# The one-hots of eight tokens: three VectorE operations over 1024 columns instead of nine small ones on VectorE and four on POOL

## What is computed

```python
def peer_ffn(h, wq, subkeys, u_tab, v_tab):
    q = (t @ wq).reshape(ntok, 8, 2, 128)
    sc = jnp.einsum('thpd,hpkd->thpk', q, subkeys)
    s1, i1 = lax.top_k(sc[:, :, 0], 16)
    s2, i2 = lax.top_k(sc[:, :, 1], 16)
    cand = (s1[..., :, None] + s2[..., None, :]).reshape(ntok, 8, 256)
    best, pos = lax.top_k(cand, 16)
    e1 = jnp.take_along_axis(i1, pos // 16, axis=-1)
    e2 = jnp.take_along_axis(i2, pos % 16, axis=-1)
    idx = e1 * 128 + e2
    gate = jax.nn.softmax(best, axis=-1)
    ...
    act = jax.nn.gelu(jnp.einsum('phkd,pd->phk', u_tab[ib], tb)) * gb
    return jnp.einsum('phk,phkd->pd', act, v_tab[ib])
```

## Time and profile before

| | us |
|---|---|
| median of 3 runs (lowest, highest) | 4073.61 (4067.85, 4075.52) |
| the profiled execution, its own time | 4059.55 |
| its span, first to last instruction | 4057.7 |
| PE busy in it | 3913.6 |
| DVE busy | 2264.8 |
| ACT busy | 1470.3 |
| POOL busy | 866.5 |

### The profile page before, as it was taken

One profiled execution on the slowest core, in us unless ns is written; L12 is line 12 of the kernel. 1 busy time (PEld: TensorE's weight loads), 2 busy tenths in 40 slices (PEclk: granted clock), 3 DMA queues, 4 the chain that ended last, 5 costly groups with the idle time before them and its releaser, 6 DMA issues. The chain is left out here.

```text
span 4057.7 us, 55604 instructions
## 1 busy us (share of the span) xinstructions
PE 3913.6 (96%) x22292; PEld 3412.3 (84%) x22292; DVE 2264.8 (56%) x3948; ACT 1470.3 (36%) x2122; POOL 866.5 (21%) x780
## 2 busy tenths in 40 slices
PE   8999999999899999999899999999999999999998
PEld 7987799999785668788677886699999999999998
DVE  4434446554544445555557543367997665666665
ACT  3253335222325344422355343333333333333333
POOL 1000012112100002211103500026656553111100
PEclk9999999999999999999999999999999999999999
DMA  3111132222110113222122121236656778888874
GB/s 130 61 39 42 42 115 94 90 93 89 58 64 35 50 52 128 91 96 97 63 89 63 32 94 55 87 112 215 221 172 203 248 247 290 281 265 265 266 251 138
DMA packets 232559, 519.42 MB, mean 128 GB/s; under 512 B 36272, under 2 KB 134704, under 8 KB 231920
## 3 DMA queue, kind: packets, MB, share of 16 engines
q1 hardware_dynamic: 160288, 399.71, 29.8%
q0 software_dynamic: 18432, 67.12, 4.7%
q10 hardware_dynamic: 53584, 49.04, 3.6%
HBM read 454.66 MB, written 60.82 MB: 127 GB/s over the span
## 5 line engine op out<-in xcount | busy, mean ns | idle before, releaser
L304 PE MATMUL PSM<-UX,PARTS 128*128 128x264 f32 (+3 forms) x3392 | 1184.0, 349 | 44.1 <-DVE UX L333 24.9
L305 PE MATMUL PSM<-UX,PARTS 128*128 128x264 f32 (+3 forms) x3392 | 1164.9, 343 | 0.0
L306 PE MATMUL PSM<-UX,PARTS 128*128 128x264 f32 (+3 forms) x3392 | 1161.4, 342 | 0.0
L272 DVE TENSOR_TENSOR PARTS<-RAW,PARTS 128x1024 fp32r<-128x1024 f32 x549 | 686.0, 1256 | 600.4 <-ACT PARTS L262 545.8
L262 ACT ACTIVATE PARTS<-RAW 128x1024 fp32r<-128x1024 f32 x612 | 644.9, 1056 | 991.6 <-PE PSM L306 485.7
L304 PEld LDWEIGHTS PSM<-UX,PARTS 128*128 128x128 f32 x3392 | 645.1, 190 | 130.7 <-DVE UX L333 34.7
L305 PEld LDWEIGHTS PSM<-UX,PARTS 128*128 128x128 f32 x3392 | 645.7, 190 | 59.1 <-issue 2.9
L306 PEld LDWEIGHTS PSM<-UX,PARTS 128*128 128x128 f32 x3392 | 644.9, 190 | 59.0
L2591 PE MATMUL PSM<-AC,PARTS 128*128 128x448 f32 x1024 | 375.3, 366 | 2.0 <-DVE AC L2850 2.0
L2593 PE MATMUL PSM<-AC,PARTS 128*128 128x448 f32 x1024 | 374.6, 366 | 0.0
L2592 PE MATMUL PSM<-AC,PARTS 128*128 128x448 f32 x1024 | 374.6, 366 | 0.0
(11 more groups left out here) (388 smaller groups left out, 5692.8 us busy)
## 6 DMA issues: line engine op xcount, KB each, us to landing
RAW<-w_ff_dram SPq DMA_DIRECT2D x128, 512.0 KB
RAW<-peer_u_dram SPq DMA_DIRECT2D x128, 512.0 KB
RAW<-peer_v_dram SPq DMA_DIRECT2D x128, 512.0 KB
RAW<-w_in_dram SPq DMA_DIRECT2D x116, 512.0 KB
acts_dram<-MQ ACTq DMA_DIRECT2D x128, 224.0 KB
MQ<-acts_dram SPq DMA_DIRECT2D x128, 224.0 KB
MQ<-gates_dram SPq DMA_DIRECT2D x128, 224.0 KB
RAW<-w_mix_o_dram SPq DMA_DIRECT2D x32, 512.0 KB
```

What stands on the lines that cost most here:

```text
L272: e.tensor_tensor(p[:, 1024:2048], self.raw.of(i), p[:, 0:1024].bitcast(F), SUB).then_inc(V.sem, V.tick("w", i))
L304: e.matmul(dst, wh[k], xh_[k][:, lo:hi], start=(k == 0), stop=False, skip_group_check=True)
L305: e.matmul(dst, wh[k], xl_[k][:, lo:hi], start=False, stop=False, skip_group_check=True)
L306: m = e.matmul(dst, wl[k], xh_[k][:, lo:hi], start=False, stop=(k == kk - 1), skip_group_check=True)
```

## The change

DVE's `one_hots` handles eight tokens at once with three tensor_tensor over 8 x 128 = 1024 columns: is_equal of iota with E1 into A, is_equal with E2 into B, then A times Gt in place. The third waits for the first by DVE's own semaphore. It waits once, for the eight before the last one (both halves). The tick "onA" of both halves is that of the third operation. POOL's `one_hots` and its call are removed, and PE's wait for them. The matmuls, buffers and the order on the other engines stay.

```diff
@@ gates (PE)
                     e.wait_ge(V.sem, V.at("onA", i4))
-                    if half:
-                        e.wait_ge(G.sem, G.at("onB", i4))
                     for i in range(4):
@@ one_hots (DVE)
-                for half in range(2):
-                    i4 = four_at(n, t8) + half
-                    a, o, t0 = onA[i4 % 4], onB[i4 % 4], 128 * n + 8 * t8 + 4 * half
-                    if i4 >= 4:
-                        e.wait_ge(T.sem, T.at("on", i4 - 4))
-                    for i in range(4):
-                        e.tensor_scalar(a[:, 128 * i:128 * i + 128], iota, E1[:, t0 + i:t0 + i + 1], Gt[:, t0 + i:t0 + i + 1],
-                                        ALU.is_equal, MUL).then_inc(V.sem, V.tick("onA", i4))
-                    if i4 % 2 == 0:
-                        e.tensor_tensor(o.rearrange("p (t n) -> p t n", t=4), iota.unsqueeze(1).to_broadcast([128, 4, 128]),
-                                        E2[:, t0:t0 + 4].unsqueeze(2).to_broadcast([128, 4, 128]), ALU.is_equal).then_inc(
-                                            V.sem, V.tick("onA", i4))
+                i4, t0 = four_at(n, t8), 128 * n + 8 * t8
+                a, o = (qb(oOn + 2048 * w + 512 * (i4 % 4), 1024).rearrange("p (t n) -> p t n", t=8) for w in range(2))
+                each, of = (lambda ap: ap[:, t0:t0 + 8].unsqueeze(2).to_broadcast([128, 8, 128])), (
+                    iota.unsqueeze(1).to_broadcast([128, 8, 128]))
+                if i4 >= 4:
+                    e.wait_ge(T.sem, T.at("on", i4 - 3))
+                e.tensor_tensor(a, of, each(E1), ALU.is_equal).then_inc(V.sem, V.tick())
+                e.tensor_tensor(o, of, each(E2), ALU.is_equal).then_inc(V.sem, V.tick())
+                e.wait_ge(V.sem, V.n - 1)
+                e.tensor_tensor(a, a, each(Gt), MUL).then_inc(V.sem, V.tick("onA", i4))
+                V.mark("onA", i4 + 1)
@@ peer_pool (POOL)
-            def one_hots(n, t8):
-                i4 = four_at(n, t8) + 1
-                o, t0 = onB[i4 % 4], 128 * n + 8 * t8 + 4
-                ...
-                for i in range(4):
-                    e.tensor_scalar(o[:, 128 * i:128 * i + 128], iota, E2[:, t0 + i:t0 + i + 1], None,
-                                    ALU.is_equal).then_inc(G.sem, G.tick("onB", i4))
...
-                for n, t8 in gates_at(i):
-                    one_hots(n, t8)
```

## The result

The changed kernel takes 4077.25 us (median of 12 runs), the kernel before, in 12 runs beside it, 4066.13. The ratio is 1.0033, 95% interval 1.0017 to 1.0048: slower by a third of a per cent. By the ratio that is 13 us, with an interval from 7 to 20; the two medians lie 11.1 apart. The prediction was 4087.2 in a range of 4073 to 4101, 13.6 us over a median of 4073.61; the difference came out as forecast, and the level lies lower because before's median came down with more runs. Rival A's 4.4 us and rival B's 3.2 lie outside the interval, and so, just, does C's 20.8. Single runs of one kernel lie up to 23 us apart (4052.61 to 4075.91 for before), so the place of a gain or loss has to be read inside a trace.

What follows compares the result with a forecast made beforehand. PE sets the pace inside a block (8.43 us a step), DVE 4% behind; DVE becomes the bound of three blocks. Block delays 1.7 + 4.8 + 2.7 + 4.4 = 13.6 us on the 4073.61 median give 4087.2, range 4073 to 4101.

Steps and rivals of the forecast that it cites:

- Rival A: Between blocks: delays recovered there, only the last block's 4.4 us left, 4078.0 us; chance 0.14.
- rival B: DVE's port: quiet POOL lets each tensor_tensor pass in 1.07 us or less, loss 3.2 us, 4076.8; chance 0.08.
- C: Inner waits (4.2 us) and low clock after head waits (3.0) added to the sum: 20.8 us, 4094.4; chance 0.18.
- The price of an operation: DVE's one-hots: each 1024-column tensor_tensor takes 1.13 us, 3.39 for eight tokens, 6.78 a step.
- A step with a dot: DVE in a block: halving 1.13, dot 1.24 and one-hots 6.78 make 9.15 us, against PE's 8.43.
- The blocks: The four blocks running the changed code (32 steps): their ends come later by 13.6 us in sum.
- n=3: Block of steps 70 to 73, no dots, PE the bound: 1.7 us later.
- n=2: Block of steps 112 to 119, five steps with a dot, DVE the bound: 4.4 us later.
- n=0: Block of steps 80 to 87, five steps with a dot, DVE the bound: 4.8 us later.
- n=1: Block of steps 96 to 103, DVE the bound, PE already waiting 3.23 us at its head: 2.7 us later.
- The cover between the blocks: Gaps between blocks: PE busy 36.0 of 36.0 us, so no idle time swallows a delay; each handed on whole.
- POOL at nothing: Removing POOL's 224 tensor_scalar takes nothing off the path, and its gathers are costed at nothing.

Runs made afterwards that it cites:

- after_again: Changed kernel, unedited, traced a second time: 406.7 us from PE's end of the tile of step 70 to the first peer_v matmul.
- the third trace: Changed kernel, unedited, traced a third time: 405.1 us from PE's end of the tile of step 70 to the first peer_v matmul.
- before_again: Kernel before, unedited, traced a second time: 388.5 us from PE's end of the tile of step 70 to the first peer_v matmul.
- wide_a_pool_b: Kernel before with A made by two 1024-column tensor_tensor on DVE, B still shared with POOL: 1.0176 times the kernel before.

## Why the prediction was right, step by step

**The price of an operation.** 1.13 forecast, 1.14 measured for all three forms; durations of L2787, L2788 and L2790 lie between 1204 and 1225 ns over 168 operations. A step with a dot 9.15 forecast, 9.09 measured (the dot takes 1.14, not 1.24). The dot of the earlier trace rows, 1.30 us long, was not the usual one: of the 15 dots inside the blocks of before, six lasted 1.30 and nine 1.21, while all in the blocks of the changed kernel last 1.21 to 1.22. The other four steps with a dot in the block of the earlier trace rows took DVE 7.91 to 7.97 us, not its 8.12, so up to 0.5 us was to spare. A step without a dot was forecast at 7.91 and took 7.95.

**The blocks.** Forecast 1.7 + 4.8 + 2.7 + 4.4 = 13.6 us against one trace; means of three 2.3, 3.7, 4.3, 4.8. Three terms were mis-sized. n=3 is 0.6 longer: the sum took PE's three steps at 8.43, but one of them holds the transposes for n=2 (its group starts 8.76 after the last one, before and after), and PE starts 0.2 us later than the spacing of DVE's starts says, since it waits for the end of the last operation (1.21, not 1.13) and some 0.15 more. n=0 is 1.1 shorter: DVE starts 2.4 to 2.9 us ahead of PE's end of the tile in the changed kernel, where I took the 0.9 of the one trace of before. n=1 is 1.6 longer, and that is before's side: its first trace had the latest of three heads (69.0 us against 65.5 and 66.9), which made the block look as if it had less to lose. For the length of the block after I had 3268.9 - 3197.2 = 71.7, and 71.4 came. The errors cancel, and the 13.6 is nearer to 15 than its parts deserve.

**The cover between the blocks.** Named as none, and nearly so: DVE's starts at n=1 and n=2 moved with the block's end, which rules out rival A there. At n=0 DVE starts 1.2 us earlier than in before, for a reason that no run separates; in all six traces DVE's halving there waits for ACT's rounding of the tile. **Rival B** (the port): the relief is real, 0.025 us for a tensor_scalar, and misses the operations of the change: they took 1.14, where B needed 1.07 or less. **Rival C**: the inner wait costs nothing, since another operation stands in between; the full wait costs what the rows said. The low clock did not come at n=3 and n=0, with waits of up to 1.8 us. It came after the waits of 3.1 to 4.6 us at n=1 and n=2 in all three traces of the changed kernel, as the stretches of after_again at n=1 and of the third trace at n=2 show:

```profile
3205.00:3207.00 2.00, 2.00 (x10) 2.00 (x11) 2.00 (x3) 0.97 (x2) 0.00 (x0) 0.50 1.06 398
3326.00:3331.00 5.00, 4.23 (x21) 3.96 (x20) 5.00 (x7) 0.00 (x0) 1.09 (x1) 0.50 0.84 276
```

The wait's length alone doesn't decide it: in before_again the clock was 0.50 after 1.76 us at n=2 (3311 to 3313), and 1.00 after the 1.78 us at n=3 here. The gate group then lasts 5.43 to 7.16 us. But 5.43 is also what a first group lasts at n=3 and n=0 at the full clock, where PE waits 1.38 us for its second eight. PE's timeline of after_again, n=0 and n=1:

```profile
3090.14 2.02 PE L2565 MATMUL PSM<-MQ 128*128 128x128 f32 x16 [1.06 <-DVE MQ L2790]
3093.54 2.02 PE L2565 MATMUL PSM<-MQ 128*128 128x128 f32 x16 [1.38 <-DVE MQ L2790]
3204.77 5.43 PE L2565 MATMUL PSM<-MQ 128*128 128x128 f32 x32 [3.67 <-DVE MQ L2790]
```

The slow matmuls fill a wait that was there anyway, and where they last longer PE catches up with DVE within the block: from DVE's start the blocks of n=1 and n=2 take 70.8 to 71.3 us, those of n=0, without the low clock, 70.7 to 70.8. So it costs the changed kernel 0.5 us a block at most, as C said of the blocks in which DVE is the bound.

**POOL at nothing.** Right for the change as it is: no wait for POOL existed, and the 34 gathers from step 75 on, which now take 1.34 us in the mean instead of 1.20, are late for nobody. As a general statement ("the form doesn't count, DVE's load does") it was wrong, and my expectation for wide_a_pool_b shows it: with the wide operations on DVE, POOL's share would have become the bound. Taking it off POOL is the condition on which the wide form costs 0.3% and not 1.8%.

## What to carry to other kernels

Add up an engine's starts over one step of the pipeline and compare with the pace of the bound: with 0.3 to 0.5 us of 8.4 to spare, two thirds of one more microsecond went to the end in each step with a dot (9.09 against 8.43), however low the engine's share of the span is. When work moves between VectorE and GpSimd, price both with the new neighbour: an operation's mean from the old kernel holds only beside the operations it ran with. And where a bound engine waits at the head of a block, look for the work that could start a step earlier before looking at its size; then for what is late next.

## What the runs showed of the hardware

- POOL's tensor_scalar over 128 columns took 590 ns at the least in before and in wide_a_pool_b, 854 in the mean beside DVE's small operations and 1241 beside its wide ones, with medians of 602 and 610 and a longest of 9.02 us beside a train of wide ones; a wide in-place operation on DVE took 1304 in the median beside it and 1212 without it.
- DVE's tensor_scalar came 0.255 us apart without POOL's work, 0.28 with it.
- A wait of VectorE for its own instruction just before added 0.11 us; one for the instruction before that added nothing.
- Three traces of one kernel differ by up to 5.0 us in the stretch (before, 388.5 to 393.5) and by up to 2.7 in where DVE stands at a head (before, n=1). Why the head of n=0 comes 1.2 us earlier in the changed kernel was not settled.
